# Later and earlier places in a hand-timed plan, and the mixed rows' stores moved from SyncE's queue to GpSimd's

## The chip, the cores and the metric

One core of one Trainium2 chip runs the whole kernel. The metric is device microseconds (us) of one execution, from start to end; lower is better. Engines are named as the profile names them: PE is TensorE (PEld its weight loads), ACT is ScalarE, DVE is VectorE, POOL is GpSimd, SP is SyncE. SP computes nothing here, it only issues DMAs.

## The reference, cut to what matters

One layer of a hybrid attention block over a sequence of 1024 rows of width 1024. Three groups of eight heads share one input projection; each group has another kind of attention; the result, gated, goes through an output projection and is added to the input.

```python
h = rmsnorm(x, norm_g)
proj = h @ w_in                       # per group q, k, v, gate (512 columns each), 8 forget logits
o_sb = stick_breaking_attention(...)  # group 0, strictly causal, sigmoids, no softmax
o_ch = chunked_relpos_attention(...)  # group 1, softmax over own chunk + 8 before, relative bias
o_fx = forgetting_attention(...)      # group 2, causal softmax with cumulative log-forget bias
mixed = concat(o_sb * silu(g_sb), o_ch * silu(g_ch), o_fx * silu(g_fx))
out = x + mixed @ w_out               # mixed: 1024 x 1536, w_out: 1536 x 1024
```

## The kernel before, in words

All matmuls are made of split operands: a value is a high part (float32r) and a low part (the rest), and a product is three matmuls. So most tiles are written twice, first by ACT (the high part, a copy) and then by DVE (the low part, a subtraction that reads what ACT wrote).

The 24 heads are worked in 12 pairs `j`, in the order group 1 (pairs 0 to 3), group 2 (4 to 7), group 0 (8 to 11). A pair has 16 blocks of query rows, `n = 16 j + r`, eight for each of its two heads. The unit of the schedule is such a block, one "step", about 4.7 us long in the profile.

The order of all work is one list, `PLAN`, that `plan()` writes. Every piece has a due time in steps, written by hand in `AT` (pieces of a block), `OWN` (pieces of the pair `j` itself) and `NEXT` (pieces that prepare pair `j + 1`); `extras()` collects the ones of a block, the list is sorted by time, and the projection matmuls of the next pair are strewn between as filler. Pieces that cost PE nothing do not shift the filler. Each engine then walks through `PLAN` and carries out only its own part of each piece, strictly in that order, with semaphore waits between engines. So a piece's due time sets its place in the queue of every engine that has a part in it, and whatever stands behind a waiting instruction on the same engine waits too.

The pieces that matter here:

- `scores` (PE, L1290 and L1291, into `psS`): query block times keys. Then DVE adds the bias and takes the row minimum (L1114, L1123, into `z`) for the softmax groups, or ACT takes two sigmoids (L924, L925) for group 0. PE may start the scores of block `n` only when DVE (or ACT) has read those of `n - 1`, if either is wide, else of `n - 2`.
- `diag` (POOL, L771): for group 2 a masked copy of the bias block on the diagonal, which DVE needs in the same block's L1123. It waits for the DVE pass of block `n - 2`. Due at `n - 0.6`.
- `weigh`, `recip`, `rescale`: the exponential (ACT L933), the reciprocal (DVE L1132), the scaling (ACT L939). In group 0 `weigh` is a scan and a product on DVE (L1146, L1149).
- `turn` and `values`: PE transposes four weights blocks (L1307, `psT`), ACT and DVE evacuate them into `pt` (L949, L1157), PE multiplies with the values (L1325).
- `sq` and `norm`: the squares of q and k (ACT L879, DVE L1044, L1047), a power -0.5 on POOL (L754, two instructions), the scaling (DVE L1053, two instructions for each head), then `heads`: PE transposes (L1264), ACT and DVE evacuate into `stack` (L891, L1062), SP issues two copies inside `stack` (L658, L659). `keys`: SP waits until these copies have landed and issues two more (L665, L666); the scores of the second four blocks of the head need them. `('keys', 0, 1)`, the first head's second half, is due at 2.4 and used by the scores of block `r = 4`.
- `weights` and `gatew`: the next pair's columns of `w_in`. SP loads them (L600) three pieces ahead into slots of `wraw`. For `weights` ACT scales and copies (L813) and DVE subtracts (L1007). For `gatew`, the gate's columns, POOL first multiplies by the norm's gain (L763, and waits for the load), ACT copies (L821, waits for POOL), DVE subtracts (L1019). `gatew` is due at 6.3 and 7.3 of each pair that has a next one.
- `gather` and `mix`: the output of a head times its gate (DVE L1164, L1170). For pair `j - 1` the half `u` of the mixed rows is split in step `16 j + 2.25` (`u = 0`) and `16 j + 6.25` (`u = 1`): ACT copies the high part to `mst` (L968), DVE subtracts (L1176, counts `s_mlo`), and SP waits for `s_mlo` and stores both to DRAM (L676, 24 of each, 256 KB each). ACT's next copy into `mst` waits for the store. The last two are stored in the end phase, and read back from DRAM (`tail`, L725; `full`, L709) for the last products (L1373).
- In the first pair only: `skew` (SP, L636), six copies in DRAM that spread a bias row over 128 rows, needed by `bias` of pair 1 on; and `forget`, `decay`, the second half of the cumulative forget gate: a transpose (PE L1273), three small ACT functions on 8 partitions (L906, L908, L910), DVE (L1079, L1085, a scan L1087, L1091), and SP's store (L670).

POOL's order of pieces is that of `PLAN` too, with a wait for its own previous piece ahead of each: in pair 5 of before, for example, `sq 5,1` (80.2), `diag 81` (80.4), `diag 82`, ..., `diag 87` (86.4), `gatew 6,0` (86.3, ahead of `diag 87`), `gatew 6,1` (87.3).

Of the kernel before, what the change touches and what calls it, by code (L numbers as in the profile page):

```python
# [30 lines left out]
HALF = 512  # L31
# [23 lines left out]
def group(n):  # L55
    return GRP[n // (16 * PPG)]
# [97 lines left out]

AT = {'diag': -0.6, 'tail': 0.3, 'weigh': 0.85, 'recip': 0.9, 'rescale': 1.65, 'turn': 1.35, 'turns': 3.05, 'gather': 0.5, 'mix': 2.25}

OWN = {('sq', 1): 0.2, ('norm', 1, 0): 1.0, ('norm', 1, 1): 2.2, ('heads', 0, 1): 1.75, ('keys', 0, 1): 2.4, ('heads', 1, 0): 4.6, ('keys', 1, 0): 5.5, ('keys', 1, 1): 9.5, ('vsplit', 0, 1): 5.6, ('vsplit', 1, 1): 6.6, ('heads', 1, 1): 8.6}
NEXT = {('weights', 0): 0.2, ('weights', 1): 0.6, ('weights', 2): 1.1, ('weights', 3): 1.6, ('weights', 4): 2.1, ('weights', 5): 2.6, ('weights', 6): 3.1, ('weights', 7): 3.6, ('gatew', 0): 6.3, ('gatew', 1): 7.3, ('sq', 0): 10.3, ('norm', 0, 0): 11.7, ('norm', 0, 1): 12.3, ('heads', 0, 0): 13.4, ('keys', 0, 0): 14.3, ('vsplit', 0, 0): 13.9, ('vsplit', 1, 0): 15.5}  # L160

BEHIND_TURN = {('weights', 2): 1.5, ('weights', 3): 1.9, ('weights', 4): 2.3}

WOUT = [round(0.6 + 0.6 * c, 2) for c in range(SOON)] + [round(4.2 + 0.35 * c, 2) for c in range(EARLY - SOON)]
FIRST_AT = 3.2
MIXF = [1.1, 2.9, 4.3, 7.0]
RESIDUAL = [0.3, 7.7, 9.7]
LAST = 19
FORGET = {("forget", 1): 6.0, ("decay", 1): 7.0}
REST = {"t": 0, "g": 0, "f": 0}  # L170


def extras(j, r):
    found = [(at % 1, (kind, j, *rest)) for (kind, *rest), at in OWN.items()
             if at // 1 == r and (kind != "sq" or 0 < j < NORMED)]
    if j + 1 < PAIRS:
        ahead = NEXT if j < PPG else {**NEXT, **BEHIND_TURN}
        found += [(at % 1, (kind, j + 1, *rest)) for (kind, *rest), at in ahead.items()
                  if at // 1 == r and (kind != "sq" or j + 1 < NORMED)]
    if r == 8 and j + 1 < NORMED:  # L180
        found.append((0.7, ("bias", j + 1, 0)))
    if r == 0 and 0 < j < NORMED:
        found.append((0.7, ("bias", j, 1)))
    if j == 0:
        found += [(at % 1, step) for step, at in FORGET.items() if at // 1 == r]
    if j == 0 and 1 <= r <= 6:
        found.append((0.7, ("skew", r + 1)))
    if j == PAIRS - 1:
        found += [(at % 1, ("residual", c)) for c, at in enumerate(RESIDUAL) if at // 1 == r]
        found += [(at % 1, ("mixF", t)) for t, at in enumerate(MIXF) if at // 1 == r]  # L190
        found += [(at % 1, ("wout", c)) for c, at in enumerate(WOUT) if at // 1 == r]
    return found


def turned_steps(u):

    seq = [("turn", u, 0)]
    for b in range(1, len(banks(u))):
        seq += [("turn", u, b), ("values", u, b - 1)]
    return seq + [("values", u, len(banks(u)) - 1)]  # L200
# [37 lines left out]
def plan():  # L238
# [37 lines left out]
    for n in range(NB + 8):  # L276
        j, r, u = n // 16, n % 16, n // 4
        if n < NB:
            timed.append((n, ("scores", n)))
            if group(n) == 2:  # L280
                timed.append((n + AT["diag"], ("diag", n)))
            timed.append((n + AT["weigh"], ("weigh", n)))
            timed += [(n + f, s) for f, s in extras(j, r)]
        if n < NSOFT:
            timed.append((n + AT["recip"], ("recip", n)))
            timed.append((n + AT["rescale"], ("rescale", n)))
        if r % 4 == 0 and 0 < u <= UNITS:
            seq = turned_steps(u - 1)
            first, span = n + AT["turn"], AT["turns"]
            timed += [(first + i * span / len(seq), s) for i, s in enumerate(seq)]  # L290
        if r % 4 == 0 and 2 <= u:
            timed.append((n + AT["gather"], ("gather", u - 2)))
            if u >= 3 and (u - 2) % 4 >= 2:
# [85 lines left out]
def last_turn(step):  # L379
    return TURN0[step] + turns_of(step)  # L380
# [6 lines left out]
def build(nc, x, norm_g, w_in, b_forget, q_norm_ch, k_norm_ch, q_norm_fox, k_norm_fox, rel_bias, w_out, out):  # L387
# [4 lines left out]
    mix_d = nc.dram_tensor("mixed_scratch", (2, TT, P, PAIRS, P), F32).ap()  # L392

    with ExitStack() as ctx:
        def sb(name, shape, dt=F32):
            return ctx.enter_context(nc.sbuf_tensor(name, shape, dt))

        def sem(name):
            return ctx.enter_context(nc.semaphore(name))
# [32 lines left out]
        gate = sb("gate", [P, 2, SEQ])  # L432
# [4 lines left out]
        mst = sb("mst", [P, HALF])  # L437
# [3 lines left out]
        diag = sb("diag", [P, 2, P])  # L441
# [90 lines left out]
        s_mlo = sem("s_mlo")  # L532
        s_mix = [sem("s_mix0"), sem("s_mix1")]
# [34 lines left out]
        def by_head(rows, u):  # L568
            return rows[:, 16 * u:16 * u + 16].rearrange("p (t f s) -> p t f s", t=4, f=2)

        def bias_loads(n):
            return n // 16 + 1
# [4 lines left out]
        def _(sp):  # L577
# [44 lines left out]
            for step in PLAN:  # L622
                kind = step[0]
# [10 lines left out]
                if kind == "skew":  # L634
                    _, hd = step
                    sp.dma_start(skew_d[hd], rev_d[hd:hd + 1, :].broadcast_to([P, REVW])).then_inc(s_skew, 16)  # L636
                if kind == "bias":
                    _, j, s = step
# [6 lines left out]
                    if j < PPG:  # L645
                        if j == 1 and s == 0:
                            sp.wait_ge(s_skew, 16 * HG)
                        src = bass.AP(skew_d[hd].tensor, hd * P * REVW + P - 1, [[REVW - 1, P], [1, P * WIN]])
# [4 lines left out]
                if kind == "heads":  # L653

                    _, j, s, u = step
# [4 lines left out]
                if kind == "keys":  # L660

                    _, j, s, u = step
# [4 lines left out]
                if kind == "decay":  # L667
                    _, u = step
                    sp.wait_ge(s_fc, 2 * u + 1)
                    sp.dma_start(decay_d[:, u * HALF:(u + 1) * HALF], mst[0:HG, :]).then_inc(s_fdma, 16)  # L670
                if kind == "mix":
                    _, j, u = step
                    i = 2 * j + u
                    sp.wait_ge(s_mlo, i + 1)
                    for h, src in enumerate((mst[:, :], gate[:, j % 2, u * HALF:(u + 1) * HALF])):
                        sp.dma_start(mix_d[h, 4 * u:4 * u + 4, :, j, :].rearrange("t p q -> p t q"),  # L676
                                     src.rearrange("p (t q) -> p t q", t=4)).then_inc(s_mix[u], 16)
                if kind == "mixF":
                    _, t = step
                    if t == 0:  # L680
# [18 lines left out]
                if kind == "full":  # L699
                    _, t = step  # L700
# [26 lines left out]
                if kind == "result":  # L727
                    t, c = ENDS[step[1]]
# [4 lines left out]
        @block.gpsimd  # L733
        def _(pool):
            nc.gpsimd.memset(ident_raw, 0.0).then_inc(s_const, 1)
            pool.wait_ge(s_const, 1)
            nc.gpsimd.affine_select(out=ident_raw, in_=ident_raw, compare_op=ALU.not_equal, fill=1.0,
                                    base=0, pattern=[[-1, P]], channel_multiplier=1).then_inc(s_const, 1)
            nc.gpsimd.memset(mhalf[:, :], -0.5).then_inc(s_const, 1)
            nc.gpsimd.memset(rb[:, :, SEQ:SEQ + 1], 0.0).then_inc(s_const, 1)  # L740
            done = {"const": s_const, "square": s_rs, "sq": s_rn, "norm": s_qc, "gatew": s_gmul, "diag": s_diag}
            for step in PLAN:
                kind = step[0]
                if step in POOL_BEHIND:
                    pool.wait_ge(done[POOL_BEHIND[step][0]], POOL_BEHIND[step][1])
                if kind == "square":
                    _, t = step
                    pool.wait_ge(s_ms, t + 1)
                    nc.gpsimd.tensor_tensor(xs[:, t, 1:2], xs[:, t, 0:1], mhalf[:, 0:1], ALU.pow).then_inc(s_rs, 1)
                if kind == "sq":  # L750
                    _, j, u = step
                    pool.wait_ge(s_ss, 2 * j + u + 1)
                    for s in range(2):
                        nc.gpsimd.tensor_tensor(by_head(rs, u)[:, :, :, s], by_head(ms, u)[:, :, :, s], by_head(mhalf, 0)[:, :, :, s],  # L754
                                                ALU.pow).then_inc(s_rn, 1)
                if kind == "gatew":
                    _, j, h = step
                    c = CHUNK[step]
                    w = wplace[CSLOT[c]].rearrange("p (k c) -> p k c", k=4)
                    pool.wait_ge(s_wld[CSLOT[c]], 16 * CUSE[c])  # L760
                    if c < KT + 2:
                        pool.wait_ge(s_gcol, 16)
                    nc.gpsimd.tensor_tensor(w, w, gcol[:, 4 * h:4 * h + 4].rearrange("p (k a) -> p k a", a=1).broadcast_to(  # L763
                        [P, 4, P]), ALU.mult).then_inc(s_gmul, 1)
                if kind == "diag":

                    n = step[1]
                    s, b = n // TT % 2, n % TT
                    pool.wait_ge(s_bias[s], 16 * bias_loads(n))
                    pool.wait_ge(s_z, n - 1)  # L770
                    nc.gpsimd.affine_select(out=diag[:, n % 2, :], in_=rb[:, s, b * P:(b + 1) * P], compare_op=ALU.is_gt,  # L771
                                            fill=BIG, base=1, pattern=[[-1, P]], channel_multiplier=1).then_inc(s_diag, 1)
                if kind == "norm" and step[1] >= NORMED and step[3] == 0:
                    _, j, u, _ = step
                    pool.wait_ge(s_raw, TT * j + 4 * u + 4)
                    for s in range(2):
                        pool.wait_ge(s_turn, last_turn(("heads", j - 1, s, u)))
                    nc.gpsimd.tensor_copy(qk_out(0, u), qk_raw(0, u))
                    nc.gpsimd.tensor_copy(qk_out(1, u), qk_raw(1, u)).then_inc(s_qc, 1)
# [618 lines left out]
```

## Time and profile before

| | us |
|---|---|
| median of 3 runs | 1036.41 (1034.72 to 1042.01) |
| the profiled execution, its own time | 1036.77 |
| its span, from first to last instruction | 1035.0 |
| PE busy in the span | 1003.0 |
| DVE busy | 697.9 |
| ACT busy | 630.7 |
| POOL busy | 124.0 |

The span is 1.8 us shorter than the execution's own time; what lies around it is not in the trace. Busy time is the union of an engine's instructions; an idle time stands in the trace in front of the instruction that waited, with the engine and line that released it. A timeline row gives start, length, engine and line, and, in brackets, the idle time just before with its releaser. SP and all DMA issues are marked with a q, and their length is the issue, not the transfer.

### The profile page before, as it was taken

How to read it: one execution, taken by the hardware profiler on the slowest of the kernel's cores; microseconds unless marked ns; L12 is line 12 of the kernel's file. 1: busy time of each engine (PE TensorE's matmuls, PEld its weight loads, DVE VectorE, ACT ScalarE, POOL GpSimd, SP SyncE). 2: the span in 40 equal slices, each digit the busy share in tenths (PEclk: the TensorE clock that was granted, in tenths of full speed). 3: DMA queues.
4: the chain of work that ended last, by engine and by line, in shares of the span. 5: the costliest groups of instructions: out<-in, count | busy, mean ns of one | idle time of the engine just before them, and what ended most of it. 6: DMA issues, size and time to landing. Idle time of an engine off the chain costs nothing.

```text
span 1035.0 us, 16364 instructions
## 1 busy us (share of the span) xinstructions
PE 1003.0 (97%) x5688; PEld 910.0 (88%) x5688; DVE 697.9 (67%) x1418; ACT 630.7 (61%) x1230; POOL 124.0 (12%) x152
## 2 busy tenths in 40 slices
PE   6999999999999999999999999999999999999998
PEld 6988989899899898998998998998998997787887
DVE  5665675765855766866767657979879888877100
ACT  6658775766766767767757768657666556553000
POOL 1310201101202122121111110102002010000000
PEclk9999999999999999999999999999999999999999
DMA  8244152342431522522513414314304218732920
GB/s 253 83 133 126 29 140 63 87 110 55 120 97 29 140 77 57 133 57 69 128 49 82 123 28 102 83 35 108 77 21 119 74 52 251 201 128 78 348 98 36
DMA packets 118066, 105.51 MB, mean 102 GB/s; under 512 B 10048, under 2 KB 94024, under 8 KB 117984
## 3 DMA queue, kind: packets, MB, share of 16 engines
q1 hardware_dynamic: 115904, 104.43, 36.5%
q8 instruction: 45, 0.74, 0.3%
q10 hardware_dynamic: 2080, 0.04, 0.1%
q14 instruction: 37, 0.30, 0.1%
HBM read 62.44 MB, written 19.98 MB: 80 GB/s over the span
## 4 chain that ended last, share of the span: by engine, by line
PE 73%; DVE 13%; DMA 5%; ACT 4%; issue 3%; SPq 1%; POOL 1%; POOLq 0%; DVEq 0%; ACTq 0%
PE psP L1242 37%; PE psO L1325 7%; PE psT L1307 6%; PE psS L1290 4%; PE psS L1291 4%; PE psP L1373 3%; PE psS L1373 3%; PE psP L1246 2%; DMA stack<-stack 2%; DVE big L1007 2%; PE psP L1343 2%; DVE pt L1157 2%; PE psO L1373 2%; DVE rb L1146 2%; PE psT L1264 1%
## 5 line engine op out<-in xcount | busy, mean ns | idle before, releaser
L1242 PE MATMUL psP<-big 128*128 128x384 f32 (+1 forms) x2304 | 474.5, 344 | 1.8 <-DVE big L1007 1.3
L1242 PEld LDWEIGHTS psP<-big 128*128 128x128 f32 x2304 | 396.4, 188 | 9.7 <-DVE big L1007 1.6
L1157 DVE TENSOR_TENSOR pt<-psT,pt 128x512 fp32r<-128x512 f32 (+1 forms) x224 | 143.3, 640 | 117.8 <-ACT pt L949 116.7
L949 ACT ACTIVATE pt<-psT 128x512 fp32r<-128x512 f32 (+1 forms) x224 | 124.7, 557 | 103.3 <-PE psT L1307 102.8
L1246 PE MATMUL psP<-big 128*128 128x512 f32 x576 | 155.9, 403 | 0.0
L1325 PE MATMUL psO<-pt,vst 128*128 128x512 f32 (+3 forms) x576 | 138.1, 339 | 8.3 <-DVE pt L1157 7.3
L1307 PE MATMUL psT<-identr,z 128*128 128x128 f32 x816 | 125.2, 272 | 0.0
L1325 PEld LDWEIGHTS psO<-pt,vst 128*128 128x128 f32 x576 | 100.5, 188 | 23.5 <-issue 9.3
L1246 PEld LDWEIGHTS psP<-big 128*128 128x128 f32 x576 | 102.3, 189 | 17.9
L1307 PEld LDWEIGHTS psT<-identr,z 128*128 128x128 f32 x816 | 102.7, 140 | 15.7
L1290 PE MATMUL psS<-stack 128*128 128x256 f32 (+3 forms) x288 | 97.4, 346 | 5.0 <-DMA stack<-stack 4.6
L939 ACT ACTIVATE z<-z,small 128x640 f32<-128x640 f32 (+7 forms) x128 | 93.4, 730 | 2.7 <-DVE small L1132 2.4
L933 ACT ACTIVATE z<-z,small 128x640 f32<-128x640 f32 (+7 forms) x128 | 93.2, 728 | 2.8 <-DVE small L1123 2.8
L1291 PE MATMUL psS<-stack 128*128 128x256 f32 (+3 forms) x288 | 94.9, 332 | 0.0
L1146 DVE TENSOR_TENSOR_SCAN rb<-rb,diag 128x128 f32<-128x128 f32 (+3 forms) x64 | 86.2, 1348 | 0.0
L754 POOL TENSOR_TENSOR rs<-ms,mhalf 128x8 f32<-128x8 f32 x32 | 53.6, 1692 | 251.2 <-DVE ms L1047 251.2
L856 ACT ACTIVATE raw<-psP 128x384 f32<-128x384 f32 x88 | 43.1, 490 | 61.6 <-PE psP L1242 60.9
L924 ACT ACTIVATE rb<-psS 128x128 f32<-128x128 f32 (+3 forms) x64 | 41.7, 652 | 54.1 <-PE psS L1291 54.1
L1007 DVE SCALAR_TENSOR_TENSOR big<-wraw,gcol,big 128x384 fp32r<-128x384 f32 x90 | 55.6, 620 | 12.3 <-ACT big L813 11.8
L1290 PEld LDWEIGHTS psS<-stack 128*128 128x128 f32 x288 | 54.2, 188 | 10.3 <-DMA stack<-stack 5.8
L813 ACT ACTIVATE big<-wraw,gcol 128x384 fp32r<-128x384 f32 x90 | 54.7, 611 | 11.4 <-DMA wraw<-in_w_in_dram 11.1
L1291 PEld LDWEIGHTS psS<-stack 128*128 128x128 f32 x288 | 54.4, 189 | 3.9
(114 smaller groups left out, 1128.8 us busy)
## 6 DMA issues: line engine op xcount, KB each, us to landing
stack<-stack SPq DMA_DIRECT2D x192, 128.0 KB, 2.3
wraw<-in_w_in_dram SPq DMA_DIRECT2D x90, 192.0 KB, 2.6
wraw<-in_w_in_dram SPq DMA_DIRECT2D x24, 256.0 KB, 3.7
mixed_scratch<-mst SPq DMA_DIRECT2D x24, 256.0 KB, 2.3
mixed_scratch<-gate SPq DMA_DIRECT2D x24, 256.0 KB, 3.0
wraw<-in_w_out_dram SPq DMA_DIRECT2D x24, 256.0 KB, 3.2
rb<-decay_scratch SPq DMA_DIRECT2D x8, 512.0 KB, 4.1
big<-mixed_scratch SPq DMA_DIRECT2D x8, 512.0 KB, 5.7
```

Of the source, the lines that this page charges most:

```text
L933: nc.scalar.activation(z[:, at:at + w], z[:, at:at + w], ACT.Exp, scale=-1.0, bias=small[:, q, 0:1], accum_out=small[:, q, 2:3]).then_inc( ...
L939: nc.scalar.activation(z[:, at:at + w], z[:, at:at + w], ACT.Copy, scale=small[:, n % 8, 3:4]).then_inc(s_pn, 1)
L949: nc.scalar.activation(pt[:, ci % PTR, 0, 0:w], psT[:, m % NT, 0:w], ACT.Copy).then_inc(s_hi, 1)
L1146: nc.vector.tensor_tensor_scan(out=back, data0=back, data1=own[:, SEQ - w:SEQ][:, ::-1], initial=0.0, op0=ALU.mult, op1=ALU.max).then_inc( ...
L1157: nc.vector.tensor_tensor(pt[:, ci % PTR, 1, 0:w], psT[:, m % NT, 0:w], pt[:, ci % PTR, 0, 0:w].bitcast(F32), ALU.subtract).then_inc(s_eva ...
L1242: ins = nc.tensor.matmul(dst[:, 0:TOKW - first], hT[a][:, k, i * P:(i + 1) * P], wpair[b][:, k, first:TOKW], start=(k == 0 and q == 0), st ...
L1246: ins = nc.tensor.matmul(dst[:, :], wpair[b][:, k, TOKW:WP], hT[a][:, k, i * HALF:(i + 1) * HALF], start=(k == 0 and q == 0), stop=(k == K ...
L1290: nc.tensor.matmul(dst, qs, stack[:, s, 1, key:key + w], start=True, stop=False)
L1291: ins = nc.tensor.matmul(dst, qs, stack[:, s, 2, key:key + w], start=False, stop=True)
L1307: ins = nc.tensor.transpose(psT[:, m % NT, col:col + P], z[:, at:at + P], ident)
L1325: ins = nc.tensor.matmul(psO[:, q0 * P:(q0 + cnt) * P], vst[:, (2 * j + s) % 3, kb, :], pt[:, ci % PTR, v, col:col + cnt * P], start=(b == ...
L1373: ins = nc.tensor.matmul(shaped(endbank[g % 5], wo[b][k][c]), src[:, a, :], wo[b][k][c], start=(k == k00 and q == 0), stop=(k == PAIRS - 1 ...
```

## The change

Five edits of places in the plan, and one of the issuing engine:

- `diag` is due at `n - 0.9` in place of `n - 0.6`.
- In the pairs from the second on, `('keys', 0, 1)` is due at 2.05 in place of 2.4.
- The second `forget` is due at 3.7 in place of 6.0, its `decay` at 4.9 in place of 7.0.
- The six `skew` copies of the first pair are due at 2.7 to 7.7 in place of 1.7 to 6.7.
- The stores of `mix` are issued by POOL, at the same place of the plan, in place of SP, with the same wait for `s_mlo`.

The block that goes stands in SP's walk through `PLAN`, the one that comes in POOL's, behind `diag`.

```diff
-AT = {'diag': -0.6, 'tail': 0.3, 'weigh': 0.85, 'recip': 0.9, 'rescale': 1.65, 'turn': 1.35, 'turns': 3.05, 'gather': 0.5, 'mix': 2.25}
+AT = {'diag': -0.9, 'tail': 0.3, 'weigh': 0.85, 'recip': 0.9, 'rescale': 1.65, 'turn': 1.35, 'turns': 3.05, 'gather': 0.5, 'mix': 2.25}
...
+KEYS_AT = 0.05
...
-FORGET = {("forget", 1): 6.0, ("decay", 1): 7.0}
+FORGET = {("forget", 1): 3.7, ("decay", 1): 4.9}
...
+    if j and r == 2:
+        found = [(KEYS_AT if step[0] == "keys" else at, step) for at, step in found]
...
-    if j == 0 and 1 <= r <= 6:
-        found.append((0.7, ("skew", r + 1)))
+    if j == 0 and 2 <= r <= 7:
+        found.append((0.7, ("skew", r)))
...
-                if kind == "mix":
-                    _, j, u = step
-                    i = 2 * j + u
-                    sp.wait_ge(s_mlo, i + 1)
-                    for h, src in enumerate((mst[:, :], gate[:, j % 2, u * HALF:(u + 1) * HALF])):
-                        sp.dma_start(mix_d[h, 4 * u:4 * u + 4, :, j, :].rearrange("t p q -> p t q"),
-                                     src.rearrange("p (t q) -> p t q", t=4)).then_inc(s_mix[u], 16)
...
+                if kind == "mix":
+                    _, j, u = step
+                    i = 2 * j + u
+                    pool.wait_ge(s_mlo, i + 1)
+                    for h, src in enumerate((mst[:, :], gate[:, j % 2, u * HALF:(u + 1) * HALF])):
+                        pool.dma_start(mix_d[h, 4 * u:4 * u + 4, :, j, :].rearrange("t p q -> p t q"),
+                                     src.rearrange("p (t q) -> p t q", t=4)).then_inc(s_mix[u], 16)
```

## Rows read from the trace of the kernel before

**Rows 1.** The page's part 1: busy us, share of the span, instructions of each engine.
```profile
PE 1003.0 (97%) x5688; PEld 910.0 (88%) x5688; DVE 697.9 (67%) x1418; ACT 630.7 (61%) x1230; POOL 124.0 (12%) x152
```

**Rows 2.** Waits of PE: who, for what, us in total, times, longest us.
```profile
PE psO L1325 <- DVE pt L1157: 7.3, 11, 1.8
PE psS L1290 <- DMA stack<-stack: 4.6, 6, 1.5
PE psT L1264 <- DVE qks L1053: 2.8, 4, 0.7
```

**Rows 3.** Line L763 and L676: duration ns min/median/max, first and last start us, forms.
```profile
L763 POOL TENSOR_TENSOR wraw<-wraw,gcol x24: 1039/1042/1692, 26.5 to 796.5; 128x512 f32<-128x512 f32 x24
...
L676 SPq DMA_DIRECT2D mixed_scratch<-mst x24: 370/372/525, 135.7 to 955.9; - x24
L676 SPq DMA_DIRECT2D mixed_scratch<-gate x24: 377/508/1517, 136.3 to 956.3; - x24
```

**Rows 4.** Timeline of pair 5, steps 86 to 88: start us, us, what.
```profile
434.80 0.63 ACT L821 ACTIVATE big<-wraw 128x512 fp32r<-128x512 f32 x1
...
438.83 0.37 ACT L949 ACTIVATE pt<-psT 128x256 fp32r<-128x256 f32 x1
...
436.37 0.69 DVE L1176 TENSOR_TENSOR gate<-gate,mst 128x512 fp32r<-128x512 f32 x1
...
439.65 1.07 DVE L1114 CUSTOM_DVE_ANT_0 z<-psS,rb 128x896 f32<-128x896 f32 x1
...
442.34 0.22 PE L1290 MATMUL psS<-stack 128*128 128x128 f32 x1
```

**Rows 5.** Timeline of pair 1, steps 22 to 24.
```profile
151.91 0.63 ACT L821 ACTIVATE big<-wraw 128x512 fp32r<-128x512 f32 x1
...
152.94 0.69 DVE L1176 TENSOR_TENSOR gate<-gate,mst 128x512 fp32r<-128x512 f32 x1
...
158.98 0.22 PE L1290 MATMUL psS<-stack 128*128 128x128 f32 x1
```

**Rows 6.** Timeline of pair 8, steps 134 to 136.
```profile
659.56 0.69 DVE L1176 TENSOR_TENSOR gate<-gate,mst 128x512 fp32r<-128x512 f32 x1
660.17 0.68 DVE L1019 TENSOR_TENSOR big<-wraw,big 128x512 fp32r<-128x512 f32 x1
...
664.16 0.41 DVE L1157 TENSOR_TENSOR pt<-psT,pt 128x256 fp32r<-128x256 f32 x1
...
664.63 0.50 PE L1325 MATMUL psO<-pt,vst 128*128 128x256 f32 x2
```

**Rows 7.** Timeline of pair 5, step 81, the masked bias.
```profile
407.14 3.48 POOL L754 TENSOR_TENSOR rs<-ms,mhalf 128x8 f32<-128x8 f32 x2 [8.16 <-DVE ms L1047]
...
411.21 0.35 DVE L1123 CUSTOM_DVE_ANT_0 z<-psS,diag,small 128x128 f32<-128x128 f32 x1 [1.12 <-POOL diag L771]
...
412.42 0.66 PE L1264 MATMUL psT<-identr,qks 128*128 128x128 f32 x4 [0.71 <-DVE qks L1053]
...
413.71 0.70 PE L1325 MATMUL psO<-pt,vst 128*128 128x512 f32 x2 [0.63 <-DVE pt L1157]
```

**Rows 8.** Timeline of pair 4, steps 66 to 68, the second keys.
```profile
341.94 0.60 SPq L659 DMA_DIRECT2D stack<-stack  x1
...
345.73 0.81 SPq L665 DMA_DIRECT2D stack<-stack  x1
...
350.34 0.38 PE L1290 MATMUL psS<-stack 128*128 128x256 f32 x1 [1.45 <-DMA stack<-stack]
```

**Rows 9.** Timeline of the first pair, steps 3 to 8.
```profile
72.02 1.32 PE L1242 MATMUL psP<-big 128*128 128x384 f32 x6 [1.33 <-DVE big L1007]
...
90.29 0.51 PE L1325 MATMUL psO<-pt,vst 128*128 128x256 f32 x2 [0.98 <-DVE pt L1157]
```

**Rows 10.** Timeline of the end phase: SP's store, and the read back.
```profile
943.59 0.38 SPq L676 DMA_DIRECT2D mixed_scratch<-gate  x1
946.52 2.70 SPq L725 DMA_DIRECT2D stack<-mixed_scratch  x6
```

## The prediction

> **What bounds the kernel now.** I read the page's busy times first. PE is busy for 1003.0 of 1035.0 us [rows 1], so at most 32 us could be won, and only by removing PE's waits. The waits of PE, longest in total first, say what they are [rows 2]: 7.3 us for DVE's evacuation of turned weights (L1157), 4.6 us for the copies inside `stack`, 2.8 us for the scaled q and k (L1053). About 10 us more lie at the very start, which the change does not touch. PE has no slack, and the other engines have some 30% of idle time, but in a strict order of their own, a step or two behind PE: a stall of ACT or DVE that is longer than this lag turns into a wait of PE. So I went from PE's waits to the timelines around them, and then to the timelines of every place where the change puts something new in a queue.
>
> The matmuls and their order stay (the moved pieces cost PE nothing, but for four small transposes of `forget`). All that changes is who waits.
>
> **Keys at 2.05.** At step 66 the heads' copies are issued to 342.54, but the keys' copies only at 345.73 to 347.57, because SP first waits for `mix` and issues its two stores and a weight load; PE then waits 1.45 us for them [rows 8]. The heads' copies should land some 2.3 us after their issue (the small stores' and copies' usual landing), about 344.5; the keys then go out 1.2 us earlier, and no longer behind 512 KB of stores in the same queue. That is enough for this wait, and the five others are no longer. Term: -4.6 us, all of [rows 2]'s second row. Bounds: 0 (the heads land late) and -4.6. A weight load now stands behind the keys' wait, up to 2.2 us later; it is issued three pieces ahead, so I take 0 for it.
>
> **Masked bias at -0.9.** In pair 5 POOL does the two powers (407.14 to 410.6) and only then the masked block that DVE needs; DVE loses 1.12 us, PE then waits 0.71 for q and k and 0.63 for the evacuation that DVE does next [rows 7]. At 80.1 in place of 80.4 the masked block comes ahead of `sq 5,1` (80.2). It waits for the pass of block 79, long over, so it costs the powers nothing. PE's 0.71 goes; of the 0.63 about half stays, since DVE's queue is full from there and PE arrives earlier as well. Pairs 4 to 7 each show the 0.7 (2.8 in all [rows 2]), pairs 5 to 7 the second: 2.8 + 3 x 0.35 = 3.9 us. Term: -3.9. Bounds 0 and -4.7.
>
> **The first pair.** The `skew` copies (384 KB each) no longer stand directly ahead of the first heads' copies; SP's wait in `keys` gets shorter, the last weights come earlier, and PE's 1.33 us for L1007 go [rows 9]. The second `forget` leaves step 6, where it holds up ACT and with it the evacuation: PE's 0.98 us (and a wait of 0.4 after it) go [rows 9]. But its three ACT functions, with loads of tables around the logarithm, now stand ahead of the exponential of block 3, which DVE's queue waits for, and PE's scores of block 5 wait for DVE: about 1.1 back. Term: -1.3 - 1.4 + 1.1 = -1.6. Bounds -2.7 and +2.
>
> **The stores on POOL.** SP loses 48 issues of 0.37 to 0.51 us [rows 3] and 24 waits; nothing behind them on SP is late any more (counted above). POOL gets them, and the wait with them. What is queued behind the wait on POOL? For `u = 0`, due at 2.25: in groups 1 and 0 nothing before the next `mix`; in group 2 the masked block of 16 j + 4, needed some 6 us later. Cost 0. For `u = 1`, due at 6.25, the next piece is `gatew` at 6.3: POOL's product of the gate's columns with the gain. Before, POOL did it as soon as the load had landed, well ahead of ACT's need. Now it can start only when DVE has finished L1176 and both stores are issued. ACT's L821 waits for it, and everything behind it on ACT; DVE's L1019 waits for ACT. This is a new wait in 10 of the 12 pairs (1 to 10: the first has no `mix`, the last no `gatew`).
>
> Its price: call the time of POOL for one store D. ACT's L821 can start at (end of L1176) + 2 D + 1.04 us, the product's median [rows 3].
>
> D: the trace has no DMA issued by POOL. Lower end: 0 (a hand-over). Nearest issue rows: SP's 0.37 and 0.51, 0.88 for both [rows 3]. A store is 512 pieces of 512 bytes; POOL's own pass over a tile of this very shape takes 1.04 us [rows 3], and with its work done in software I take that: D = 1.04. Upper end, twice that, 2 us. The Trainium skill ("DMA: Bandwidth & Descriptors", Specifications) has about 1 us to the first byte for a DMA from GpSimd against 0.6 for one from SyncE. No row here shows a DMA from POOL; an estimate of D = 1 by it would give the same sum within 1 us.
>
> *Group 2, pair 5* [rows 4]: L1176 ends at 437.06, so ACT's L821 starts at 437.06 + 2.08 + 1.04 = 440.18 in place of 434.80, 5.4 us late. ACT then has L821, a copy, a scaling, an evacuation and an exponential to do before L949 (3.0 us of work), which starts at 443.2 in place of 438.83; DVE's L1157 follows 0.4 later, then the bias pass of block 87 (1.07 and 0.35, before at 439.65), which ends at 445.5. PE's scores of block 88 need it and started at 442.34: 3.2 us of new wait. Four pairs: 12.8.
>
> *Group 1, pair 1* [rows 5]: L1176 ends 153.63, L821 starts at 156.8 in place of 151.91. The same chain, with a block of 640 columns, takes 4.5 us from there to the end of block 23's pass, 161.3; PE's scores of block 24 started at 158.98: 2.3 us. Three pairs: 6.9.
>
> *Group 0, pair 8* [rows 6]: L821 can start at 660.25 + 3.12 = 663.4, DVE's L1019 at 664.05 in place of 660.17, 3.9 late. DVE has no idle time here, so L1157 (before 664.16 to 664.57) ends 3.9 later, and PE's values, which start at 664.63, wait 3.8. Three pairs (8, 9, 10): 11.4.
>
> Sum for D = 1.04: 31.1. The slope is 2 us for each us of D in each of ten pairs: D = 0 gives 10.2, D = 0.44 (SP's issue) 19, D = 2 gives 50.
>
> **The end.** Before, the store of `mix 11,0` was issued to 943.97 and SP's read back of it started at 946.52 [rows 10]; its last piece lands close to 952, just when PE wants it (the chain that ended last has the product at 952.33). POOL's two stores end about 1.0 later: +0.6 us. Bounds 0 and +3.
>
> **Sum.** -4.6 - 3.9 - 1.6 + 31.1 + 0.6 = +21.6. On the profiled execution's own 1036.8 us: 1058.4. That execution is 0.4 us above the median of the runs, so I say 1058.
>
> **The rivals.**
> - *Cheap hand-over.* POOL issues as fast as SP, D = 0.44: 19 - 10.1 + 0.1 = +9, 1046. For: the transfer itself is done by the DMA engines. Against: D stands in no row of POOL, whose shortest pass over 128 columns takes 0.3.
> - *Only the order costs.* D near 0, loss 10.2, gain 10.1: 1037, no change. The wait for L1176 alone makes the loss.
> - *The wait never reaches PE.* ACT and DVE have enough idle time and the gains remain: 1036.8 - 10.1 = 1027. For: ACT is idle for 39% of the span [rows 1]. Against: [rows 6], where L1157 ends 0.06 us before PE reads it, with DVE full ahead of it. It decides for the change only if the lag behind PE absorbs over 3 us in all three groups.
> - *Slow descriptors.* D = 2 or more: 50.3 - 10.1 + 1 = +41, 1078. What could make it so is DVE, whose instructions run next to POOL's: L763 takes 1.04 us mostly and 1.69 at most [rows 3]. The Trainium skill ("SBUF — State Buffer", the "DVE blocks DMA" trap) says that a DMA from GpSimd gets no descriptors while VectorE runs in a 2-port mode. By its section "Practical consequences" VectorE's `tensor_tensor`, most of DVE's work at these places, has no such mode; so I do not make it the forecast. The 1.69 fits its rule on reads, and no row here shows descriptors being starved.
>
> **How the numbers follow.** Forecast 0.50, cheap hand-over 0.20, slow descriptors 0.14, only the order 0.10, the wait never reaches PE 0.06. A measurement of this kernel can tell about 1% from no change, that is 10 us: the first three are slower by over 1% except for half of the cheap case's band, which I leave with 0.04 in "same"; that makes slower 0.80, same 0.14, faster 0.06. The range leaves out the last case and half of the slow one: 1036 to 1080. Within the forecast's own case D between 0.8 and 1.4 gives 1053 to 1066.
>
> **What would show it.** In the profile of the changed kernel: a new row in the waits, ACT L821 for POOL L763, ten times, about 4 to 5 us each; L1019 on DVE idle behind ACT; PE waiting for L1157 or for L1114/L1123 around the 7th step of pairs 1 to 10, 2 to 4 us each, about 31 in all. PE's waits for `stack` and for L1053 should be gone, as should DVE's wait for `diag`. I am wrong if ACT's L821 still finds POOL done, or if POOL's product stands right behind L1176 with D under 0.3; the gains are wrong if PE still waits for `stack`.

## The result, and the profile after

The changed kernel takes 1080.39 us (median of 6 runs, 1076.91 to 1082.73) against 1037.18 us for the kernel before, measured beside it; the ratio is 1.042, 95% interval 1.040 to 1.044. Slower, as forecast, but by 43 us where 21.6 were forecast, and 0.4 us above the upper end of the range (1080).

The profiled execution has a span of 1078.6 us, 43.6 more than before. Where they lie is read first from the page's part 1 and the row of PE's granted clock in part 2 (the span in 40 slices, in tenths of full speed):

```profile
span 1078.6 us, 16364 instructions
...
PE 1018.6 (94%) x5688; PEld 921.8 (85%) x5688; DVE 697.7 (65%) x1418; ACT 630.4 (58%) x1230; POOL 158.1 (15%) x200
...
PEclk9999999999999999999999899899999999999999
```

PE makes the same 5688 matmuls but is busy 15.6 us longer than in [rows 1]: the clock was lower for part of the time (a mean of 0.986; 1.000 before). So the 43.6 us are 15.6 us of slower matmuls and 28.0 us of more idle time. The waits are below, of all engines and then of PE (who, for what, us in total, times, longest us). Most lines stand four further down than in the kernel before: L1161 is its L1157, L1180 its L1176, L1023 its L1019, L825 its L821. L760 is its L763.

```profile
ACT big L825 <- POOL wraw L760: 48.1, 12, 5.1
PEld psO L1329 <- DVE pt L1161: 42.2, 22, 4.7
PE psO L1329 <- DVE pt L1161: 37.6, 26, 4.4
DVE big L1023 <- ACT big L825: 36.8, 10, 4.1
...
ACT big L817 <- DMA wraw<-in_w_in_dram: 25.4, 13, 3.9
...
PE psS L1294 <- DVE small L1127: 4.6, 7, 1.8
PE psS L1294 <- DMA stack<-stack: 2.5, 3, 1.6
```

Ten of the twelve waits of ACT for GpSimd's product are new, 3.7 to 5.1 us each, and DVE waits behind ACT ten times. PE's wait for `pt` went from 7.3 to 37.6 us [rows 2]. The wait for `stack` went from 4.6 only to 2.5 (three waits, in pairs 1 to 3), and the row of the scaled q and k (L1053 before) is gone. There is one row that the forecast did not look for: ACT waits 25.4 us for weights.

GpSimd's instructions by line show the price of a store issued there:

```profile
L760 POOL TENSOR_TENSOR wraw<-wraw,gcol 128x512 f32<-128x512 f32 x24 | 25.4, 1060 | 14.7 <-DMA wraw<-in_w_in_dram 13.5
...
L775 POOL DMA_DIRECT2D mixed_scratch<-mst x24 | 18.9, 787 | 298.4 <-DVE gate L1180 298.4
L775 POOL DMA_DIRECT2D mixed_scratch<-gate x24 | 18.0, 751 | 0.5 <-issue 0.5
```

So a store takes GpSimd 0.79 and 0.75 us, in place of the 1.04 that the prediction took. The transfers land 3.4 and 4.1 us after the issue, where SyncE's took 2.3 and 3.0 (the page's part 6).

The place of [rows 4], pair 5, in the timelines of POOL, ACT, DVE and PE (start, length, engine and line, in brackets the idle time before and its releaser):

```profile
444.75 0.77 POOL L775 DMA_DIRECT2D mixed_scratch<-mst  x1 [5.60 <-DVE gate L1180]
445.51 0.75 POOL L775 DMA_DIRECT2D mixed_scratch<-gate  x1
446.28 1.05 POOL L760 TENSOR_TENSOR wraw<-wraw,gcol 128x512 f32<-128x512 f32 x1
...
447.86 1.04 POOL L760 TENSOR_TENSOR wraw<-wraw,gcol 128x512 f32<-128x512 f32 x1
...
447.42 0.63 ACT L825 ACTIVATE big<-wraw 128x512 fp32r<-128x512 f32 x1 [5.11 <-POOL wraw L760]
...
450.49 0.36 ACT L953 ACTIVATE pt<-psT 128x256 fp32r<-128x256 f32 x1
...
443.76 0.69 DVE L1180 TENSOR_TENSOR gate<-gate,mst 128x512 fp32r<-128x512 f32 x1
448.09 1.35 DVE L1023 TENSOR_TENSOR big<-wraw,big 128x512 fp32r<-128x512 f32 x1 [3.63 <-ACT big L825]
...
451.37 0.51 PE L1329 MATMUL psO<-pt,vst 128*128 128x256 f32 x2 [2.24 <-DVE pt L1161]
...
452.92 0.30 PE L1294 MATMUL psS<-stack 128*128 128x128 f32 x1 [0.51 <-DVE small L1127]
453.06 0.28 PE L1295 MATMUL psS<-stack 128*128 128x128 f32 x1
453.17 3.73 PE L1246 MATMUL psP<-big 128*128 128x384 f32 x12
```

Read from the top: DVE ends L1180 at 444.45, GpSimd makes two stores and the product, ACT starts 5.11 us after it was free, and PE loses 2.24 us at the values (L1329), which need DVE's L1161, and 0.51 us at the scores. The last line is the second loss: 12 projection matmuls in 3.73 us. In the same pair of the kernel before, 12 of them took 2.27 us:

```profile
435.11 2.27 PE L1242 MATMUL psP<-big 128*128 128x384 f32 x12
```

In windows of this place and of its like in group 0 (us, PE busy and instructions, granted clock, DMA share, GB/s):

```profile
449.00:459.00 10.00, 7.25 (x34) 0.83 0.16 40
684.00:702.00 18.00, 13.58 (x66) 0.81 0.18 51
```

Both had a clock of 1.00 before. The trace has eight stretches at 0.5 of the clock, 1.2 in place of 2.4 GHz: seven of 3.4 us and one of 6.8. Half of their length is lost, 15.4 us in all.

### The profile page after: what moved, and what is told of

It is laid out like the page before. It is cut to its first block, busy times and chain, and to the rows that moved or that the text cites. A ratio compares the mean times of both kernels' runs of the same rounds, so it can differ in the third digit from the quotient of the medians.

```text
span 1078.6 us, 16364 instructions
## 1 busy us (share of the span) xinstructions
PE 1018.6 (94%) x5688; PEld 921.8 (85%) x5688; DVE 697.7 (65%) x1418; ACT 630.4 (58%) x1230; POOL 158.1 (15%) x200
## 3 DMA queue, kind: packets, MB, share of 16 engines
q1 hardware_dynamic: 90560, 91.84, 30.9%
q0 software_dynamic: 3840, 12.59, 4.0%
## 4 chain that ended last, share of the span: by engine, by line
PE 63%; DVE 15%; ACT 7%; DMA 6%; issue 5%; POOL 2%; SPq 1%; ACTq 0%; DVEq 0%; POOLq 0%
PE psP L1246 30%; PE psO L1329 6%; PE psT L1311 5%; PE psP L1250 4%; PE psS L1294 3%; PE psS L1295 3%; DMA wraw<-in_w_in_dram 3%; PE psP L1377 3%; PE psS L1377 3%; DVE pt L1161 2%; DVE big L1011 2%; DVE rb L1150 2%; PE psO L1377 2%; PE psP L1347 1%; PE psT L1268 1%
## 5 line engine op out<-in xcount | busy, mean ns | idle before, releaser
L1246 PE MATMUL psP<-big 128*128 128x384 f32 (+1 forms) x2304 | 485.6, 350 | 0.4 <-DVE big L1005 0.4
L1246 PEld LDWEIGHTS psP<-big 128*128 128x128 f32 x2304 | 407.0, 193 | 8.1 <-DVE big L1005 1.0
L1161 DVE TENSOR_TENSOR pt<-psT,pt 128x512 fp32r<-128x512 f32 (+1 forms) x224 | 143.4, 641 | 121.3 <-ACT pt L953 120.1
L1329 PE MATMUL psO<-pt,vst 128*128 128x512 f32 (+3 forms) x576 | 139.4, 342 | 38.4 <-DVE pt L1161 37.6
L1329 PEld LDWEIGHTS psO<-pt,vst 128*128 128x128 f32 x576 | 100.5, 189 | 55.9 <-DVE pt L1161 42.2
L1250 PEld LDWEIGHTS psP<-big 128*128 128x128 f32 x576 | 102.3, 189 | 18.0
L817 ACT ACTIVATE big<-wraw,gcol 128x384 fp32r<-128x384 f32 x90 | 54.8, 612 | 25.7 <-DMA wraw<-in_w_in_dram 25.4
L1294 PEld LDWEIGHTS psS<-stack 128*128 128x128 f32 x288 | 54.7, 190 | 14.6 <-DVE small L1127 3.9
L775 POOL DMA_DIRECT2D mixed_scratch<-mst x24 | 18.9, 787 | 298.4 <-DVE gate L1180 298.4
```

What stands on the lines that cost most here:

```text
L1161: nc.vector.tensor_tensor(pt[:, ci % PTR, 1, 0:w], psT[:, m % NT, 0:w], pt[:, ci % PTR, 0, 0:w].bitcast(F32), ALU.subtract).then_inc(s_eva ...
L1246: ins = nc.tensor.matmul(dst[:, 0:TOKW - first], hT[a][:, k, i * P:(i + 1) * P], wpair[b][:, k, first:TOKW], start=(k == 0 and q == 0), st ...
L1250: ins = nc.tensor.matmul(dst[:, :], wpair[b][:, k, TOKW:WP], hT[a][:, k, i * HALF:(i + 1) * HALF], start=(k == 0 and q == 0), stop=(k == K ...
L1294: nc.tensor.matmul(dst, qs, stack[:, s, 1, key:key + w], start=True, stop=False)
L1329: ins = nc.tensor.matmul(psO[:, q0 * P:(q0 + cnt) * P], vst[:, (2 * j + s) % 3, kb, :], pt[:, ci % PTR, v, col:col + cnt * P], start=(b == ...
```

## The experiments

Eight runs ask which part of the change does it, three what can be made of it, one where the clock's share comes from. Each was measured beside the kernel before, whose median moved between 1034.45 and 1037.18 us from one set of runs to the next. So runs of different sets are compared by their ratios.

**Plan only.** The changed kernel with the `mix` stores given back to SyncE.

```diff
-                    pool.wait_ge(s_mlo, i + 1)
...
+                    sp.wait_ge(s_mlo, i + 1)
...
```

> The changed kernel with the stores of the mixed rows given back to SyncE; the moved places of the plan stay. If the stores' place in GpSimd's queue is the cause of the loss, ACT's waits for GpSimd (ten of 3.7 to 5.1 us) and the falls of the clock behind them are gone and the time is 1031 to 1038 us, with what is left of PE's waits around the late weight loads (1.7 and 2.5 us in steps 100 and 116). If the moved places cost a good part of the 43 us (the weight loads behind the keys' wait), it stays at 1045 us or more.

1035.39 us against 1035.24, ratio 0.9993 (0.9981 to 1.0006). The moved places together are worth nothing that can be told from zero: the 10 us that they were to win are not there either. PE's waits for `stack` and L1053 are gone, but the one for `pt` grew:

```profile
PE psO L1329 <- DVE pt L1161: 13.8, 22, 1.6
PE psT L1218 <- DVE qks L987: 8.0, 2, 7.5
PE psS L1294 <- DVE small L1127: 2.0, 2, 1.8
```

(The 8.0 is the start of the kernel, the same in all.)

**Stores only.** The kernel before, its `mix` block moved to POOL's walk, nothing else.

> The kernel before with nothing changed but the stores, issued by GpSimd. If they are the cause, this alone is as slow as the changed kernel or nearly: 1070 to 1082 us, with ten waits of ACT for GpSimd of 3.7 to 5.1 us and 6 to 8 stretches of lower clock. If the loss needs the moved places too, it is under 1060 us.

1085.75 us, ratio 1.0477 (1.0443 to 1.0510). The stores alone make the whole loss, and somewhat more than I gave as its upper end. They cost 0.6% more here than in the changed kernel (1.042), so beside them the moved places may be worth some 6 us; where these would come from was not looked into. ACT's waits for GpSimd are the same ten, 3.7 to 5.1 us, with seven falls of the clock. Here PE also waits 8.2 us for `stack` (4.6 before):

```profile
PE psO L1325 <- DVE pt L1157: 33.5, 23, 4.4
PE psS L1290 <- DMA stack<-stack: 8.2, 9, 1.9
```

**Wait only.** The kernel before, with SyncE issuing the stores, and GpSimd only waiting at that place.

```diff
+                if kind == "mix":
+                    _, j, u = step
+                    pool.wait_ge(s_mlo, 2 * j + u + 1)
```

> The kernel before, with GpSimd only waiting for the mixed rows at their place of the plan, and SyncE issuing the stores as before. It parts the wait from the issue. If the order in GpSimd's queue makes the loss, ACT still waits for GpSimd ten times, each 1.5 us less than with the two stores (0.77 and 0.75 us), so 2.1 to 3.6 us; PE's new waits are 0.7 (group 1), 1.3 (group 2) and about 2.4 us (group 0), 15 us in all, and the clock falls three times at most: 1050 to 1058 us. If the issue of the stores by GpSimd is what costs (software descriptors, the slower transfer), the time is that of before, 1037 us.

1052.53 us, ratio 1.0153 (1.0126 to 1.0179). A wait instruction alone costs 16 us by the ratio, 17 between the medians. In the profiled execution PE is idle for 11.7 us more than before and busy for 5.1 us longer. ACT at the place of pair 5:

```profile
443.60 0.63 ACT L824 ACTIVATE big<-wraw 128x512 fp32r<-128x512 f32 x1 [3.35 <-POOL wraw L763]
```

3.35 in place of 5.11: the two stores are the other 1.76 (their 1.52 and what lies between). The clock fell twice, once of them behind a wait for `stack` in pair 4 and not behind GpSimd.

**Behind the gate's columns.** All 48 stores on GpSimd, those of the second halves behind the products L763 in place of ahead of them.

```diff
+                late = kind == "gatew" and step[2] == 1 and step[1] >= 2
+                if late or (kind == "mix" and not (step[2] == 1 and step[1] + 2 < PAIRS)):
+                    j, u = (step[1] - 2, 1) if late else step[1:]
...
```

> The kernel before, with the stores issued by GpSimd, but those of the second halves placed in its queue behind the two products of the gate's columns instead of ahead of them. If it is the order, ACT never waits for GpSimd and the time is 1034 to 1040 us though all 48 stores are made by GpSimd. If the stores from GpSimd are slow or disturb DVE and the other transfers in themselves, it stays at 1050 us or more.

1040.86 us, ratio 1.0048 (1.0027 to 1.0069). The order was the loss: 45 of the 50 us of "stores only" are back. ACT's ten waits are gone. What is left, half a per cent, is just above the range I gave. PE waits more for `stack`, as it did in "stores only", and not in "wait only" (5.1):

```profile
PE psS L1291 <- DMA stack<-stack: 8.0, 8, 1.7
```

So with the stores on GpSimd the copies inside `stack` land later. The second of the two `keys` copies (L666 of before) takes over 4 us from issue to landing in 10 of 48 cases here and in 11 of 48 in "stores only", against 1 before and 2 in "wait only". Whether this is the transfers' sharing of the DMA engines was not tried by itself. (The profiled execution is the slowest of the seven, 1045.09 us: PE also waited 3.4 us for L1008 at 70 us, 1.3 before, and the clock fell behind it.)

**The four moved places, each alone** on the kernel before.

```diff
-AT = {'diag': -0.6, ...
+AT = {'diag': -0.9, ...
```

> The kernel before with the masked bias at n - 0.9 alone. By the prediction's term PE's four waits for the scaled q and k (2.8 us in all) go and half of the three waits for the evacuation behind them: 3.9 us less idle time of PE, ratio 0.996. If DVE's queue only moves the wait, the idle time falls by less than 1.5 us.

1032.09 against 1036.26, ratio 0.9959 (0.9938 to 0.9979). As predicted: -4.2 us for -3.9. PE's waits for the scaled q and k are gone, and the 0.63 us behind them became 0.36.

```diff
+    if j and r == 2:
+        found = [(KEYS_AT if step[0] == "keys" else at, step) for at, step in found]
```

> The kernel before with the second keys' copies at 2.05 alone, stores on SyncE. The prediction took 4.6 us off and nothing for the weight load that now stands behind the keys' wait. If that load is late instead, ACT waits about 3 us for weights in steps 19, 35, 51, 99 and 115, PE waits 1.4 and 1.6 us for the evacuation in steps 100 and 116, and the sum is -1 to +4 us. By the prediction ACT's waits for weights stay as before (at most 1.8 us) and the ratio is 0.995.

1041.10, ratio 1.0054 (1.0036 to 1.0072): +5.6 us by the ratio, where the prediction had -4.6. PE's waits for `stack` are gone, and ACT waits 23.8 us for weights in place of 11.1, up to 4.2 at once. (The profiled execution, 1046.67 us, is one of the slowest; in "plan only", 1033.43 us, ACT waits 20.6 us for them.) It does so in steps 67, 83, 99 and 115 above all; in the first three pairs it is 1.2 to 1.5 us, so my list of steps was off. Pair 6, SP's queue, then ACT and PE (L662 is a copy of the heads, L668 and L669 are the keys, L679 the stores, L603 the weight loads):

```profile
489.67 0.60 SPq L662 DMA_DIRECT2D stack<-stack  x1
490.31 0.59 SPq L603 DMA_DIRECT2D wraw<-in_w_in_dram  x1
492.52 0.46 SPq L668 DMA_DIRECT2D stack<-stack  x1
493.02 0.60 SPq L669 DMA_DIRECT2D stack<-stack  x1
493.66 0.59 SPq L679 DMA_DIRECT2D mixed_scratch<-mst  x1
494.30 0.57 SPq L679 DMA_DIRECT2D mixed_scratch<-gate  x1
494.92 2.01 SPq L603 DMA_DIRECT2D wraw<-in_w_in_dram  x3
...
498.83 0.61 ACT L816 ACTIVATE big<-wraw,gcol 128x384 fp32r<-128x384 f32 x1 [3.17 <-DMA wraw<-in_w_in_dram]
...
500.73 0.50 PE L1328 MATMUL psO<-pt,vst 128*128 128x256 f32 x2 [1.83 <-DVE pt L1160]
```

Three weight loads leave in a row behind the keys and the stores; in the kernel before, one of them stood ahead of the keys. ACT's evacuation stands behind the late one. PE's 0.41 us for `stack` at this place of the kernel before became 1.83 us for `pt`.

```diff
-FORGET = {("forget", 1): 6.0, ("decay", 1): 7.0}
+FORGET = {("forget", 1): 3.7, ("decay", 1): 4.9}
```

> The kernel before with the second forget at 3.7 and its decay at 4.9 alone. The prediction has -1.4 us (waits at 89 to 91 us) and +1.1 us (a new wait of the scores of block 5). From the changed kernel's trace the new wait is 1.8 us: +0.4 us in all, and the wait of 1.3 us at 70.7 us stays, since it belongs to the skew copies.

1035.60, ratio 0.9992 (0.9974 to 1.0011): no change that can be told from zero. The waits at 89 to 91 us (1.4) went and 1.2 came at 78 us; the 1.3 at 71 us stayed (1.9 here).

```diff
-    if j == 0 and 1 <= r <= 6:
-        found.append((0.7, ("skew", r + 1)))
+    if j == 0 and 2 <= r <= 7:
+        found.append((0.7, ("skew", r)))
```

> The kernel before with the skew copies one step later alone. If they hold up the first heads' copies, and by them the keys' wait in SyncE's queue and the weights, PE's wait of 1.3 us for L1007 at 70.7 us goes: -1.3 us. If it is the second forget that makes that wait, it stays here and goes in the run with forget alone.

1034.00, ratio 0.9975 (0.9960 to 0.9990). The wait for L1007 at 71 us is gone. The gain by the ratio, 2.6 us, is larger than that wait, but its interval (1.0 to 4.1 us) holds 1.3 as well.

By the ratios the four add up to -2.1 us; "plan only" has -0.7 (-2.0 to +0.6). The gains of the masked bias and of the skew copies were eaten by the keys.

**PE kept busy.** The changed kernel, with transposes of the unit matrix ahead of the ten waiting products. They write a part of PSUM that is free and that nobody reads, so what is computed is the same.

```diff
+                    if b == 2 and u % 4 == 0 and 1 <= j <= 10:
+                        m = TURN0["turn", u, b] + 1
+                        for _ in range(10 if j < 4 else 12 if j < 8 else 24):
+                            nc.tensor.transpose(psT[:, m % NT, 0:P], ident, ident)
```

> The changed kernel with transposes of the unit matrix, whose result nobody reads, put into PE's queue ahead of the ten products that wait behind GpSimd (10, 12 and 24 of them in groups 1, 2 and 0, by 0.15 us each 1.5, 1.8 and 3.6 us, less than the waits). They fill PE's waits and do nothing else; DVE's chain, which ends these waits, is untouched. If the lower clock comes from PE standing still, the falls behind these waits (6 of the 8, of some 1.7 to 3.4 us each) are gone, the mean clock is over 0.995 and the time is 10 to 13 us less, 1066 to 1071 us. If the clock falls for another reason, it is 1078 us or more.

1068.85 us, ratio 1.0324 (1.0298 to 1.0349) where the changed kernel has 1.042: 150 useless matmuls take off 1%, some 10 us. (Between the two medians it is 11.5 us, but they are of different sets.) The place in pair 8, where PE stood still for 4.42 us in the changed kernel, and then its windows, this run first and the changed kernel's second:

```profile
682.58 2.78 PE L1327 MATMUL psT<-identr 128*128 128x128 f32 x24
687.16 0.51 PE L1333 MATMUL psO<-pt,vst 128*128 128x256 f32 x2 [1.79 <-DVE pt L1161]
...
688.20 2.31 PE L1246 MATMUL psP<-big 128*128 128x384 f32 x12
```

```profile
676.00:696.00 20.00, 18.13 (x118) 1.00 0.23 61
```

```profile
682.00:702.00 20.00, 15.58 (x77) 0.83 0.17 46
```

The mean clock is 0.997, with two falls in place of eight; one of the two is behind the wait in pair 4, in spite of the transposes there. The wait itself is as long as it was, 2.78 us of transposes and 1.79 us idle for 4.42 us idle: DVE ends it. Only the clock behind the waits changed: it costs 3.4 us of the profiled execution in place of 15.4.

**What can be made of it.** The two places that won alone, together; then with the keys' copies early in pairs 1 to 3 only (`if 0 < j < PPG and r == 2`); and the changed kernel whole with the stores behind the gate's columns.

> The kernel before with the two edits that won alone, the masked bias at n - 0.9 and the skew copies one step later. They act on different waits of PE (steps 65 to 114, and step 3), so they should add: 0.9959 x 0.9975 = 0.993. If the gain of either was noise, the ratio is 0.996 to 0.998.

> The same with the second keys' copies at 2.05 in pairs 1 to 3 alone. With keys early everywhere PE's waits for stack in pairs 1 to 3 (2.0 us) were gone, and its new waits for late weights stood in pairs 4 to 10 alone. So here -2 us more than the run without it, 0.991. If the weight loads of pairs 1 to 3 are late too (ACT waited 1.2 to 1.5 us for them), it is 0.993 or worse.

> The changed kernel whole, with one thing mended: GpSimd issues the second halves' stores behind the two products of the gate's columns. If the order in GpSimd's queue is the loss, the 43 us are gone but for the 5 us that the stores from GpSimd cost in the run like it without the moved places: 1036 to 1044 us. If the moved places and the stores together make more, it is over 1050 us.

Masked bias and skew: 1029.11 against 1035.76, ratio 0.9933 (0.9920 to 0.9947), the sum of the two. With the keys of pairs 1 to 3: 1026.31, 0.9914 (0.9902 to 0.9927), the best version here, faster than both kernels. Its runs (1025.94 to 1028.02) lie below those of the other (1028.30 to 1030.66). The changed kernel mended: 1037.28, 1.0021 (1.0004 to 1.0038); with one place in one queue changed it is back within 0.4% of the time before.

The best version's PE, to be held against [rows 1] and [rows 2]:

```profile
PE 1001.1 (98%) x5688; PEld 909.9 (89%) x5688; DVE 700.4 (68%) x1418; ACT 631.0 (62%) x1230; POOL 125.9 (12%) x152
```

## Why the prediction was right and wrong

*The stores on POOL, the new wait.* The mechanism was the one forecast, in the ten places forecast. Only the instruction of PE that waits is another in groups 1 and 2: the values (L1329) wait first and longest, where the prediction had the scores. In the ten places together PE's new waits are 29.1 us, for 31.1 predicted:

| | predicted each | measured each |
|---|---|---|
| group 1, three pairs | 2.3 | 1.84, 1.88, 1.84 |
| group 2, four pairs | 3.2 | 2.94, 2.75, 2.75, 2.79 |
| group 0, three pairs | 3.8 | 4.42, 3.92, 3.92 |

D was 0.77 us, not 1.04. From the end of DVE's L1180 to the start of ACT's L825 pair 5 took 2.97 us, for 3.12 predicted: the two stores took 0.56 us less, and 0.3 us ahead of the first store and 0.1 us behind the product were not in the sum. With D at nothing the prediction had 10.2 us of new waits; "wait only" is this case, and PE is idle for 11.7 us more there. In group 2 DVE's L1023 took 1.35 us beside GpSimd's next product, for 0.78 at this place before. The Trainium skill ("SBUF — State Buffer", Who interferes with whom) says that a VectorE instruction with two SBUF inputs contends with a GpSimd instruction that reads SBUF. The row bears it out: GpSimd's product (447.86 to 448.90) was there first.

*The step that failed most: "All that changes is who waits."* "Four pairs: 12.8" and its like were counted as PE's waits alone, and matmul time was taken as fixed. In the changed kernel seven of the eight waits of over 2 us were followed by matmuls at 1.2 GHz. All falls together cost 15.4 us in the profiled execution, and "PE kept busy" shows that some 10 of them come from PE's standing still and from nothing that the wait does elsewhere. Six of the eight falls, 12 us, lie behind the ten waits: with them the ten cost 41 us where 31 stood. The other two are behind PE's waits at 76 us (1.80, the moved forget's) and 590 us (2.46, the late weights').

*"I take 0 for it", of the weight load behind the keys' wait.* This is the second failure, 10 us of the sum: the keys alone cost 5.6 us, where 4.6 were to be won. I counted the wait that goes and not the load that is passed. That the load is issued three pieces ahead was no cover: ACT had waited for these loads before the change too (11.1 us in all), so there was no slack to give. The sign named for it, that PE still waits for `stack`, came true as well in the changed kernel (2.5 us), but not in "plan only" or with the keys alone: it comes with the stores on GpSimd.

*The masked bias* was right in mechanism and size: -4.2 for -3.9. *The first pair* was forecast at -1.6; skew alone has -2.6 and forget about 0, which fits the direction of both terms. *The end* (+0.6) left no wait of PE for the mixed rows in the changed kernel's trace.

*The rivals.* "Slow descriptors" named 1078, close to the time that came, but by luck: its reason is wrong, since D was less than I took, not more. "Cheap hand-over" is wrong too: D is not 0.44, and even with no store to issue (wait only) the order costs 16 to 17 us. "Only the order costs" has a part right: the order alone makes a third of the loss of "stores only" (16 of 49 us by the ratios), the issues in front of the product the rest. "The wait never reaches PE" fell in all ten places.

So the 43.6 us of the profiled execution are 29.1 of new waits, -1.1 for all that the moved places and the rest of the idle time changed, and 15.6 of longer matmuls. The prediction had 31.1, -9.5 and nothing. Of the 22 us that it missed, 15.6 are the clock and 8.4 the moved places; the waits were 2.0 too high.

## What to carry to other kernels

When a DMA's issue is moved to an engine that also computes, look at what stands behind its wait in that engine's queue; here the next piece had been ready some 5 to 10 us early, and one wait ahead of it held up two other engines and PE in turn. The same stores placed behind that piece cost a ninth as much. And price a wait of a full TensorE by its length plus the lower clock that can follow it: here 12 us on top of 29.

A wait for a transfer, put early in a queue, delays the loads behind it: try each moved place alone, since here a gain of 0.7% lay hidden in a sum of about zero.

## What the runs showed of the hardware

A store of 512 pieces of 512 bytes takes GpSimd 0.75 to 0.79 us to issue, SyncE 0.37 to 0.51, and it lands about 1.1 us later after the issue (3.4 and 4.1 us for 2.3 and 3.0). By the page's part 3 the 48 stores are 3840 packets when GpSimd issues them and 25344 when SyncE does (115904 packets on SyncE's queue before, 90560 in the changed kernel), for the same 12.6 MB.

Over the traces of all fourteen kernels PE's clock fell 26 times, counted here by the longest wait of PE around or just ahead of each fall. It fell with all seven waits of 3.4 to 4.4 us, with 9 of 16 of 2.1 to 2.6 us, with 8 of 22 of 1.7 to 2.1 us, and with 2 of 56 of 1.0 to 1.7 us. It fell to 0.5 each time, for 3.4 us in 23 cases and for 6.8 in three. The same wait of 2.24 us was followed by a fall in pair 5 of the changed kernel and by none in pairs 9 and 10 of "wait only". What decides between the two was not found.
